# Two-layer hybrid decoder trunk on one core: adding the halves of the squared row sums on VectorE before TensorE spreads them

## The reference, cut to what matters

```
def rms_norm(x, g):
    xf = x.astype(jnp.float32)
    y = xf * lax.rsqrt(jnp.mean(xf * xf, axis=-1, keepdims=True) + EPS)
    return (y * g.astype(jnp.float32)).astype(x.dtype)
...
    for l in range(DEPTH):
        h = rms_norm(x, norm1_g[l])
        proj = h @ w_in[l]
        ...
        x = x + merged @ w_out[l]
        h2 = rms_norm(x, norm2_g[l])
        x = x + jnp.square(jax.nn.relu(h2 @ w_ff1[l])) @ w_ff2[l]
    return x
```

## Time and profile before

| what | value |
|---|---|
| median of three runs | 1754.81 us (1753.19, 1754.81, 1758.35) |
| the profiled execution's own time | 1754.5 us |
| its span, first to last instruction | 1752.6 us |
| TensorE matmuls busy | 1738.7 us, 99% of the span |
| TensorE weight loads busy | 1423.2 us, 81% |
| GpSimd / VectorE / ScalarE busy | 61% / 55% / 39% |
| mean busy share of the DMA engines by slice | 0.1 to 0.7 |
| share of TensorE in the chain that ended last | 96% |

### The profile page before, as it was taken

How to read it: one execution, slowest core, us unless ns; L and a number is a source line. 1 busy time by engine, 2 the same in 40 slices (tenths; PEclk the granted TensorE clock), 3 DMA queues, 4 the chain that set the end, 5 groups by cost and what they waited for, 6 DMA issues and landing times.

```text
span 1752.6 us, 26234 instructions
## 1 busy us (share of the span) xinstructions
PE 1738.7 (99%) x9974; PEld 1423.2 (81%) x9974; DVE 963.5 (55%) x1565; ACT 691.0 (39%) x1241; POOL 1066.4 (61%) x572
## 2 busy tenths in 40 slices
PE   8999999999999999999999999999999999999999
PEld 7787888778888888878887888887788888888887
DVE  6796626653442555454576966366443435444445
ACT  6433316550104444444355243176411054444443
POOL 7554466246665777767874535662456657777776
PEclk9999999999999999999999999999999999999999
DMA  5222133122235666666442221331322356666665
GB/s 202 85 73 73 50 96 108 37 98 95 86 99 168 162 173 157 165 163 165 132 156 80 78 62 61 96 97 37 110 95 86 97 160 162 160 172 161 168 157 144
DMA packets 58896, 207.16 MB, mean 118 GB/s; under 512 B 6369, under 2 KB 8705, under 8 KB 58785
## 3 DMA queue, kind: packets, MB, share of 16 engines
q1 hardware_dynamic: 47520, 164.94, 29.8%
q0 software_dynamic: 9216, 33.56, 10.3%
q10 hardware_dynamic: 2048, 7.10, 1.1%
HBM read 184.61 MB, written 4.19 MB: 108 GB/s over the span
## 4 chain that ended last, share of the span: by engine, by line
PE 96%; ACT 1%; DVE 1%; issue 1%; DMA 0%; SPq 0%; DVEq 0%; ACTq 0%
PE ps L666 23%; PE ps L668 22%; PE ps L667 22%; PE ps L1264 6%; PE ps L1266 6%; PE ps L1265 6%; PE ps L1136 2%; PE ps L1145 1%; PE ps L1158 1%; PE ps L685 1%; PE ps L909 1%; PE ps L896 0%; PE ps L946 0%; PE ps L1208 0%; PE ps L932 0%
## 5 line engine op out<-in xcount | busy, mean ns | idle before, releaser
L666 PE MATMUL ps<-hHi,wHi 128*128 128x512 f32 x1360 | 552.9, 407 | 0.0
L668 PE MATMUL ps<-hHi,wLo 128*128 128x512 f32 x1360 | 530.3, 390 | 0.0
L667 PE MATMUL ps<-hLo,wHi 128*128 128x512 f32 x1360 | 529.8, 390 | 0.0
L566 POOL TENSOR_SCALAR wHi<-wraw 128x1024 fp32r<-128x1024 f32 x168 | 182.2, 1084 | 492.1 <-PE ps L668 475.0
L571 POOL TENSOR_TENSOR wLo<-wraw,wHi 128x1024 fp32r<-128x1024 f32 x168 | 415.7, 2475 | 13.9
L597 POOL TENSOR_TENSOR wLo<-w,wHi 128x1024 fp32r<-128x1024 f32 x96 | 237.1, 2488 | 130.7 <-ACT wHi L1695 130.5
L666 PEld LDWEIGHTS ps<-hHi,wHi 128*128 128x128 f32 x1360 | 255.4, 188 | 58.8 <-issue 6.9
L667 PEld LDWEIGHTS ps<-hLo,wHi 128*128 128x128 f32 x1360 | 255.7, 188 | 54.8 <-issue 3.8
L668 PEld LDWEIGHTS ps<-hHi,wLo 128*128 128x128 f32 x1360 | 255.3, 188 | 54.5
L1264 PE MATMUL ps<-wHi,fHi 128*128 128x512 f32 x448 | 174.4, 389 | 1.1 <-DVE y L2342 1.1
L1265 PE MATMUL ps<-wLo,fHi 128*128 128x512 f32 x448 | 174.3, 389 | 0.0
(11 more groups left out here) (337 smaller groups left out, 2671.9 us busy)
## 6 DMA issues: line engine op xcount, KB each, us to landing
wraw<-stream SPq DMA_DIRECT2D x224, 512.0 KB, 3.5
w<-stream SPq DMA_DIRECT2D x64, 512.0 KB, 4.3
w<-w POOLq DMA_DIRECT2D x32, 512.0 KB, 6.8
b<-stream SPq DMA_DIRECT2D x16, 512.0 KB, 3.5
b<-stream POOLq DMA_DIRECT2D x16, 512.0 KB, 6.1
w<-stream POOLq DMA_DIRECT2D x16, 512.0 KB, 8.3
xin<-x SPq DMA_DIRECT2D x4, 512.0 KB, 6.2
y<-x ACTq DMA_DIRECT2D x1, 2048.0 KB, 9.3
```

The source lines that it names most:

```text
L566: nc.gpsimd.tensor_scalar(wHi[:, slot], wraw[:, slot % RAW], 1.0, 0.0, ALU.mult, ALU.add).then_inc(unit_high, 1)
L666: mm(o, lh[lc], rh[rc], start=start, stop=False)
L667: mm(o, lh[lc], rl[rc], start=False, stop=False)
L668: return mm(o, ll[lc], rh[rc], start=False, stop=stop)
```

## The change

VectorE gets one more instruction for each norm, `sum_halves`: it waits until all eight row sums are there, adds the second half's four columns of `rowsq` to the first half's, and signals `rows_summed`. TensorE waits for that in place of the two waits it had, and makes four transposes in place of eight. `sum_halves` is called behind the last `stream_low` of each norm. Everything else stays.

```diff
                 def sum_stream(norm):
 
-                    pe.wait_ge(rows_squared, 8 * norm + 8)
-                    pe.wait_ge(h_lo, 8 * norm + 3)
+                    pe.wait_ge(rows_summed, norm + 1)
                     for t in range(TT):
-                        for half in range(2):
-                            last = mm(S(2)[:, t * P:(t + 1) * P], rowsq[:, half, t:t + 1].broadcast_to([P, P]), ident, start=half == 0, stop=half == 1,
-                                      is_transpose=True)
+                        last = nc.tensor.transpose(S(2)[:, t * P:(t + 1) * P], rowsq[:, 0, t:t + 1].broadcast_to([P, P]), ident)
                     last.then_inc(stat_summed, 1)
...
+            def sum_halves(norm):
+
+                dve.wait_ge(rows_squared, 8 * norm + 8)
+                nc.vector.tensor_tensor(rowsq[:, 0], rowsq[:, 0], rowsq[:, 1], ALU.add).then_inc(rows_summed, 1)
+
...
             zero_rows()
             stream_low(0)
+            sum_halves(0)
             dve.wait_ge(tables_in, 48)
...
                     stream_low(2 * layer + 1, range(4 * half, 4 * half + 4))
+                sum_halves(2 * layer + 1)
...
                     stream_low(2 * layer + 2)
+                    sum_halves(2 * layer + 2)
```

More of the change, by code:

```diff
@@ L329, in hybrid_trunk @@
         h_lo, h_high, rows_squared = sem("h_lo"), sem("h_high"), sem("rows_squared")
+        rows_summed = sem("rows_summed")
         stat_summed, rl_done, rstd_ready = sem("stat_summed"), sem("rl_done"), sem("rstd_ready")
```

## The result

The changed kernel takes 1765.84 us (median of six runs, 1765.03 to 1768.84), the kernel before 1754.84 us in the same sessions (1753.19 to 1758.35). The ratio is 1.0064 with an interval of 1.0054 to 1.0074: **11.0 us slower**, where 3.5 us were forecast. The time lies outside the range. The profiled execution is the longest of the six, 1768.84 us with a span of 1767.0 us, so its account has to explain 14.4 us of span; the median is 3.0 us shorter.

The account below looks back on a forecast made before the run. TensorE's list plus its waits was taken to bound the kernel. Norms 1 and 3 add 2.21 + 2.20 us, norms 0 and 2 save 0.44 each: 3.5 us slower, 1754.8 to 1758.3 us; range 1755.5 to 1761.8 us.

Parts of the forecast that it names:

- The wait at norms 1 and 3: Addition behind the low parts: TensorE stands still 2.65 and 2.64 us; net 2.21 and 2.20 us slower.
- The clock in these waits: Rival at norms 1 and 3: clock falls to its lower level, 1.6 us a fall; at least once 17%.
- Norms 2 and 3, the saving: Four fewer transposes save 0.44 us a norm; at norm 2, 0.8 us of matmuls cover the addition.
- The addition at norm 0: Even if held by GpSimd it ends at 19.2, before TensorE comes at 20.29; 0.44 us gained.
- The lost race: Rival at norm 0: GpSimd's next instruction goes before the addition, TensorE starts 1.5 us later, 1759.9 us; 8%.
- The steps behind the addition: Norm 0: VectorE's mask and first angles start some 2.5 us later, taken in by its 5.05 us idle time.
- The moved collision: TensorE's one 1.1 us wait for VectorE (near 775 us) may vanish or come twice: 1757.2 to 1759.4 us, within forecast.

Follow-up runs that it names:

- all four norms mended: The change at all four norms, addition ahead of the low parts at norms 1 and 3, both angle tables moved later in VectorE's list; fastest kernel: 1751.77 us.
- the wait alone: The kernel before plus one wait: VectorE waits at norm 0 for the eight row sums; no addition, eight transposes kept: 1760.3 us.
- the early addition: The change at norms 1 and 3 only, with the addition called ahead of the low parts of the blocks 4 to 7: 1752.64 us.
- norm 0 alone: The kernel before with the addition and four transposes at norm 0 only, norms 1, 2 and 3 as before: 1760.72 us.
- the first angles late: The change at norm 0 only, with the first table's angle steps moved to right ahead of the second's, near 56 us: 1756.02 us.
- scratch in PSUM: The change at norm 0 only, with the scratch tile `cyc` of the first angle table moved from SBUF to a PSUM bank: 1753.85 us.

## Why the prediction was wrong

**Where it stood.** Slower was right, and so was the mechanism of norms 1 and 3; the size was a third of what came. In the account of the 14.4 us norm 0 makes +8.8 us, for which the sum had -0.44 us, and norms 1 and 3 make some 3.7 us each, for which it had 2.2 us; the wait near 775 us gives back 1.4 and norm 2 gives 0.44.

**The wait at norms 1 and 3** was 2.65 us in the sum and 2.5 us on TensorE's weight loads in the trace, between the right events: the low parts' end, 0.15 us of addition (0.17 taken), 0.06 us to wake TensorE (0.13 taken). This step held.

**The clock in these waits** was a rival at 17%, and both pauses met it. The step that failed is the reading of the earlier trace rows: the clock stood at 1.00 for nearly 3 us after the last work, and I took from it that a pause shorter than that is safe. The rows of the changed kernel show that the fall needn't come in the pause: at norms 1 and 3 it came 0.2 and 0.7 us behind it, once TensorE was at work again. The end of a kernel can't show that. The rival's price, 1.6 us a fall from the earlier trace rows, was right (1.7 measured); its chance was not. The 64 transposes with short waits spoke only of waits much shorter than this one.

**Norms 2 and 3, the saving.** 0.44 us for a norm is confirmed where nothing else happens: the stretch from norm 2 to norm 3 is 0.39 us shorter. At norm 2 TensorE didn't wait, as said. But the addition took 0.56 us, where the sum had 0.17 and at most 0.1 for GpSimd: it began at 898.07 and a GpSimd instruction ran until 898.61, since GpSimd's instructions no longer stood where the trace of before had them. With all four norms mended it took 1.30 us and the gain went.

**The addition at norm 0** went as said too: it was held by GpSimd's instruction until 19.06, TensorE came at 20.21 and didn't wait. The lost race, at 8%, did not happen.

**The steps behind the addition** are where the sum failed. The prediction put them at nothing: "VectorE then idled 5.05 us until 24.13, and that takes it in". It priced their delay, 2.5 us, at the durations of the old place. But the duration was a property of the place. In the same paragraph I had seen the one step that touched GpSimd's next instruction, `trig`, held until its end, and had the rule of the Trainium skill (SBUF — State Buffer, section "Who interferes with whom") for it. The trace agrees with that rule as the prediction tells it, for two inputs in SBUF: 0.74 us became 4.65, and was 0.74 again with one input in PSUM. The cast (0.17 us became 2.09) and the scalar steps were held as well, as `trig` had shown. I applied what I had seen to the one instruction that the change adds, and not to the eleven that it moves. With it the danger could have been put into numbers from the rows of before: eight angle steps between SBUF tiles, each of which can lose to a GpSimd instruction of 1.05 or 2.4 us, so up to some 14 us (4 x 1.05 + 4 x 2.4, an estimate) against the 5.05 us of idle time. And behind 24.13 VectorE's busy share of 97% left nothing to take the rest.

**The moved collision** was put at 1.1 us to either side and was -1.4 us by the stretches, in every kernel but the one with the wait alone. It is the same mechanism: VectorE's low part of the second product, with both inputs in SBUF, is held by GpSimd. In the kernel before:

```profile
766.06 5.15 POOL L597 TENSOR_TENSOR wLo<-w,wHi 128x1024 fp32r<-128x1024 f32 x2
767.63 6.74 DVE L2332 TENSOR_TENSOR fLo<-mixed,fHi 128x768 fp32r<-128x768 f32 x1
770.99 2.56 POOL L597 TENSOR_TENSOR wLo<-wraw,wHi 128x1024 fp32r<-128x1024 f32 x1
```

and in the kernel with the early addition:

```profile
765.62 2.39 POOL L599 TENSOR_TENSOR wLo<-w,wHi 128x1024 fp32r<-128x1024 f32 x1 [0.40 <-ACT wHi L1702]
767.20 1.63 DVE L2348 TENSOR_TENSOR fLo<-mixed,fHi 128x768 fp32r<-128x768 f32 x1
768.19 2.90 POOL L599 TENSOR_TENSOR wLo<-w,wHi 128x1024 fp32r<-128x1024 f32 x1 [0.17 <-ACT wHi L1702]
```

VectorE comes 1.57 to 1.58 us behind the start of a GpSimd instruction in both, and in all twelve kernels. What differs is GpSimd's list. In the kernel before and in the one with the wait alone three of its instructions follow without a gap, and VectorE's ends only behind the third (774.37; 773.55). In the ten others GpSimd waits 0.16 or 0.17 us for ScalarE's `wHi` behind the first; there VectorE gets in, and GpSimd's next takes 2.9 us in place of 2.4. That this gap decides is read from the rows; no experiment tested it. So of the 2.9 us by which the best version's span is shorter, 1.4 us are this collision, which any small shift may bring back (in the second layer of the kernel with the wait alone it came new, 7.23 us); the transposes give the rest, 1.75 us less most of norm 2's share. This part of the gain is luck.

## What to carry to other kernels

When a change makes an engine wait, list everything that is queued behind the wait and price it at the new place, not by the durations of the old one: a step of 0.2 us in a neighbour's gap can be a step of 2.4 us in the neighbour's work. Look at the busy share of that engine in the tens of microseconds behind to see whether the delay can be made good. On TensorE, where it leads the kernel, count a pause with the clock fall that may follow it (here 2.5 us and 1.7 us), and put the small supporting work ahead of the work that the pause depends on.

## What the runs showed of the hardware

- **The clock can fall in a pause or just behind it, and needn't fall at all.** In the profiled executions the pauses of 2.3 us at norms 1 and 3 were followed by 3.4 us at 0.50, costing 1.7 us each; the fall came 0.2 and 0.7 us behind their end in the changed kernel. The pause of 4.5 us cost 3.4 us of clock where the fall came at its end (changed kernel, 56.0) and 2.5 us where it came 1.8 us before (norm 0 alone, 54.2); the clock was low for 6.8 us in both. Two shorter ones were followed by a fall too: 1.7 us near 65.7 with the first angles late, though in seven of ten executions the mean clock was 1.000, and 1.3 us with another of 1.0 us close behind it in the kernel with the wait alone (low from 55.1 to 58.5). Single ones of 1.0 us (scratch in PSUM) and 1.14 us were not.
- **Transposes hold the clock up** as matmuls do: behind 41 transposes in a row the granted clock was still 1.00.
- **A VectorE instruction is held until GpSimd's instruction ends, however short its own work.** One of 128x4 elements waited 2.1 us for the end, one of 128x64 2.4 us. Not only additions with two SBUF inputs are held but casts and scalar steps from SBUF to SBUF as well. Where GpSimd's instructions follow without a gap, VectorE can stand behind three of them (6.74 us). The mask, 0.21 us from 18.98, began before GpSimd's instruction at 19.14; in the kernel with the first angles late it began behind one and was held too (18.85, 1.08 us). The scalar step on 16x1 elements behind it took 0.14 us beside a running GpSimd instruction in both (19.30 and 20.02); why it is spared is open.
- **A PSUM operand frees the step**: 0.23 us beside a running GpSimd instruction.
